# A hybrid decoder step on one core: per-layer products inside an expert group, and the two last norms applied behind the products

## The reference

```python
x = x + jnp.einsum("bld,de->ble", g_a * branch_a + g_b * branch_b, w_out)
hm = _rmsnorm(x, norm_ffn).reshape(b * l, D_MODEL)
x = x + _moe(hm, w_router, ...)            # top 4 of 32 experts, clamped SwiGLU, D_FF 1024
gate = jax.nn.sigmoid(jnp.einsum("bld,de->ble", _rmsnorm(x, norm_ple), w_ple_gate))
x = x + jnp.einsum("blp,pd->bld", p_l, w_ple_proj) * gate
y = _rmsnorm(x, norm_final)                # the two first outputs
# _rmsnorm(x, g) = x * rsqrt(mean(x * x) + 1e-6) * g
```

## Time and profile before

| | us |
|---|---|
| median of 3 runs | 1566.33 |
| lowest, highest | 1565.93, 1574.47 |
| the profiled execution | 1569.91 |
| its span, first to last instruction | 1568.2 |
| TensorE busy in it | 1411.7 |
| VectorE, ScalarE busy | 502.4, 248.5 |
| mean granted TensorE clock | 0.975 |

### The profile page before, as it was taken

One profiled execution on the slowest core, in us unless ns is written; L12 is line 12 of the kernel. 1 busy time (PEld: TensorE's weight loads), 2 busy tenths in 40 slices (PEclk: granted clock), 3 DMA queues, 4 the chain that ended last, 5 costly groups with the idle time before them and its releaser, 6 DMA issues.

```text
span 1568.2 us, 19774 instructions
## 1 busy us (share of the span) xinstructions
PE 1411.7 (90%) x7420; PEld 819.7 (52%) x7420; DVE 502.4 (32%) x1084; ACT 248.5 (16%) x495; POOL 49.6 (3%) x71
## 2 busy tenths in 40 slices
PE   3899999898999999988988988989989989989877
PEld 3587777676788843442442442443443443433356
DVE  1366677777522440220220220210210211211222
ACT  2351422314230300100100100100100100100022
POOL 2010001101000000000000000000000000000000
PEclk9899989999999999999999999999999999999989
DMA  6132323232249399999999999999999999999910
GB/s 187 41 121 68 116 65 112 80 107 86 67 128 369 131 377 421 421 422 422 421 422 421 421 421 422 421 422 422 422 420 421 420 423 421 422 422 422 399 45 28
DMA packets 120448, 462.67 MB, mean 295 GB/s; under 512 B 9783, under 2 KB 68680, under 8 KB 71128
## 3 DMA queue, kind: packets, MB, share of 16 engines
q1 hardware_dynamic: 100304, 447.97, 71.2%
q10 hardware_dynamic: 20080, 13.82, 3.1%
HBM read 455.75 MB, written 6.68 MB: 295 GB/s over the span
## 4 chain that ended last, share of the span: by engine, by line
PE 63%; DMA 21%; DVE 9%; ACT 2%; issue 2%; ACTq 1%; SPq 0%; POOL 0%; DVEq 0%; POOLq 0%
DMA ring<-in_w_gate_up 21%; PE bank L996 14%; PE bank L961 12%; PE bank L799 9%; PE bank L926 6%; PE bank L1017 4%; PE bank L843 3%; PE bank L671 2%; PE bank L1068 2%; PE bank L877 2%; DVE lent L1611 2%; PE bank L954 1%; ACTq L1099 1%; PE bank L609 1%; PE bank L677 1%
## 5 line engine op out<-in xcount | busy, mean ns | idle before, releaser
L961 PE MATMUL bank<-ring,lent 128*64 128x512 f32 (+1 forms) x2304 | 459.2, 595 | 73.6 <-DMA ring<-in_w_gate_up 73.4
L961 PEld LDWEIGHTS bank<-ring,lent 128*64 128x64 f32 (+1 forms) x2304 | 149.2, 131 | 371.7 <-issue 348.5
L799 PE MATMUL bank<-lent,ring 128*128 128x264 f32 x896 | 233.9, 406 | 2.9 <-DVE big L1632 1.6
L996 PE MATMUL bank<-ring,lent 128*64 128x512 f32 (+1 forms) x1152 | 226.7, 595 | 0.2 <-ACT lent L1367 0.2
L799 PEld LDWEIGHTS bank<-lent,ring 128*128 128x128 f32 x896 | 170.1, 200 | 36.9 <-issue 7.5
L1781 DVE TENSOR_SCALAR big<-bank 128x512 f32<-128x512 f32 x32 | 20.6, 686 | 431.4 <-PE bank L961 431.4
L996 PEld LDWEIGHTS bank<-ring,lent 128*64 128x64 f32 (+1 forms) x1152 | 69.8, 131 | 135.8 <-issue 128.7
L1361 ACT ACTIVATE big<-big 128x512 f32<-128x512 f32 x32 | 19.6, 630 | 549.1 <-DVE big L1781 549.1
L926 PEld LDWEIGHTS bank<-st,big 88*128 88x128 f32 x768 | 87.0, 192 | 12.7 <-issue 12.2
L926 PE MATMUL bank<-st,big 88*128 88x128 f32 x768 | 90.0, 277 | 0.1
L1799 DVE TENSOR_TENSOR xT<-xT,bank 128x264 f32<-128x264 f32 x128 | 55.0, 430 | 95.9 <-PE bank L1017 94.4
(11 more groups left out here) (328 smaller groups left out, 1127.8 us busy)
## 6 DMA issues: line engine op xcount, KB each, us to landing
ring<-in_w_gate_up SPq DMA_DIRECT2D x256, 1024.0 KB, 19.1
ring<-in_w_down SPq DMA_DIRECT2D x128, 1024.0 KB, 23.5
ring<-in_w_in SPq DMA_DIRECT2D x28, 1024.0 KB, 5.2
st<-in_state_gdn ACTq DMA_DIRECT2D x8, 512.0 KB, 4.3
out<-st ACTq DMA_DIRECT2D x8, 512.0 KB, 3.3
ring<-in_w_gdn_out SPq DMA_DIRECT2D x4, 1024.0 KB, 5.0
ring<-in_w_out SPq DMA_DIRECT2D x4, 1024.0 KB, 9.4
ring<-in_w_ple_gate SPq DMA_DIRECT2D x4, 1024.0 KB, 16.1
```

What stands on the lines that cost most here:

```text
L799: last = mm(b[:, 0:T], w[:, k, o:o + P], aT[:, k, :], start=k == 0, stop=k == KD - 1)
L961: last = mm(bank[t][lo:hi, :], x_slots[:, c, lo:hi], w, start=False, stop=c == KD - 1)
L996: last = mm(bank[4 + t][lo:hi, :], hT[:, m, lo:hi], w, start=m == 0, stop=m == KD - 1)
```

## The change

1. The per-layer products (pp) leave the end. In group index 13 (the fourteenth of 16, `PLE_GROUP`) TensorE runs the two products of one block behind each of the eight rounds, in banks 6 and 7; ScalarE copies each out of PSUM to pieces of SBUF that are free (pp_kept), and TensorE waits for the last copy ahead of the gather. The loops of TensorE and ScalarE are cut there. w_ple_proj gets a place in `lent` and is loaded by SyncE behind expert chunk 11, once the last block of w_out is out.
2. The gate's norm: TensorE multiplies xT * gain without rstd. VectorE multiplies the product by rstd when it leaves PSUM, ahead of the sigmoid. The sum of squares runs behind the first two gate blocks.
3. The final norm: squares are summed over blocks by VectorE as they come (sum3), the column sums are taken with tokens on the partitions (ss3), and the factor is applied as ScalarE and VectorE, three copies each, take the token rows out of PSUM.
4. The final transposes are no longer behind the second norm but between the gate blocks (`final_tokens`). They are of 88 tokens, three for a block.
5. TensorE, ScalarE and VectorE read the flag ahead of the last group; the branch stays where it is.
6. ScalarE loads its tables by dummy activations ahead of use (Sqrt before the root, Sigmoid after it, Sqrt after the last sigmoid). The stores of y are issued by SyncE, eight instead of six.

```diff
+PLE_GROUP = GROUPS - 3
+        w_ple = carve(lent, 2 * D + 2 * KD * SLOTS, 2, D)
+        for i, b in enumerate((1, 5, 6, 7, 1, 0, 1, 0)):
+            plan(f"pg{i}", b)
+        for h in range(2):
+            for t in range(NTB):
+                plan(f"y{t}{h}", 2 + 3 * h + t)
+        plan("ss3", 1)
...
+            to_drain(sp, f"wo{KD - 1}")
+            sp.dma_start(w_ple, a["w_ple_proj"][0].rearrange("(k p) d -> p k d", p=P)).then_inc(s["late_loaded"], 16)
             load_group(0, 0, loaded, first, True, RING, known=True)
...
+            def per_layer(i):
+                if i >= 2:
+                    pe.wait_ge(s["pp_kept"], i - 1)
+                for k in range(2):
+                    last = mm(aux[i % 2][:, 0:T], w_ple[:, k, i * P:(i + 1) * P], pT[:, k, :], start=k == 0, stop=k == 1)
+                last.then_inc(s["pp_filled"], 1)
...
+                if ple:
+                    pe.wait_ge(s["pp_kept"], KD)
                 if not last_one:
                     gather(sm, n + 1)
...
+            most = pe.value_load(flag[0:1, 0:1], min_val=0, max_val=MOST)
             group(first, loaded, slot_fills, GROUPS - 1, EVEN, False, True, True)
             last_scatter(first, GROUPS)
-            most = pe.value_load(flag[0:1, 0:1], min_val=0, max_val=MOST)
...
+            def final_tokens(k):
+
+                pe.wait_ge(s["xg_ready"], 2 * KD + k + 1)
+                for t in range(NTB):
+                    name = f"y{t}{k // 4}"
+                    b = to_fill(pe, name) if k % 4 == 0 else bank[uses[name][0]][:]
+                    x = tr(b[0:TB, (k % 4) * P:(k % 4 + 1) * P], x3g[:, k, t * TB:(t + 1) * TB], ident[:])
+                    if k % 4 == 3:
+                        fill_done(name, x)
+
+            gate_block(0)
+            gate_block(1)
+            sum_squares("rms3", 2)
+            gate_block(2)
+            gate_block(3)
+            final_tokens(0)
+            gate_block(4)
+            final_tokens(1)
+            final_tokens(2)
+            gate_block(5)
+            final_tokens(3)
+            gate_block(6)
+            final_tokens(4)
+            gate_block(7)
+            for k in range(5, KD):
+                final_tokens(k)
+            pe.wait_ge(s["squares"], 2 * KD + 2)
+            b = to_fill(pe, "ss3")
+            pe.wait_ge(s["squares3"], KD)
...
+            for k in range(KD):
+                act.wait_ge(first["sc_added"], GROUPS * KD - KD + k + 1)
+                A(aT[:, k, :], xT[:, k, :], ACT.Copy, scale=par[:, 16 + k:17 + k]).then_inc(s["xg_ready"], 1)
+            squares(zT, lambda k: None)
+            tell(A(small8[:, 3:4], small8[:, 0:1], ACT.Sqrt, scale=0.0))
             root(rstd[:], "rms3", 1.0 / D)
+            tell(A(small8[:, 3:4], small8[:, 0:1], ACT.Sigmoid))
             for i in range(KD):
+                wait_drained(act, f"pg{i}")
+                A(ple_gate[i % 2], ple_gate[i % 2], ACT.Sigmoid).then_inc(s["ple_sig"], 1)
+                if i == KD - 1:
+                    tell(A(small8[:, 3:4], small8[:, 0:1], ACT.Sqrt, scale=0.0))
+                act.wait_ge(s["x3"], i + 1)
+                if i < KD - 1:
+                    A(x3g[:, i, :], xT[:, i, :], ACT.Copy, scale=par[:, 24 + i:25 + i]).then_inc(s["xg_ready"], 1)
+                A(sq3[i % 2] if i else sum3, xT[:, i, :], ACT.Square).then_inc(s["squares3"], 1)
...
-            norm("rms3", 16)
+            wait_drained(dve, "rms3")
+            tell(v.reciprocal(rstd[:], rstd[:]))
             for i in range(KD):
+                b = to_drain(dve, f"pg{i}")
+                x = ple_gate[i % 2]
+                out_of(v.tensor_tensor(x, b[:, 0:T], rstd[:], ALU.mult), f"pg{i}")
+                if i >= 2:
+                    dve.wait_ge(s["squares3"], i)
+                    tell(v.tensor_tensor(sum3, sum3, sq3[(i - 1) % 2], ALU.add), "squares" if i == KD - 1 else None)
+                dve.wait_ge(s["ple_sig"], i + 1)
+                tell(v.tensor_tensor(x, x, pp[i], ALU.mult))
                 tell(v.tensor_tensor(xT[:, i, :], xT[:, i, :], x, ALU.add), "x3")
-            norm("rms4", 24)
+                if i == KD - 1:
+                    dve.wait_ge(s["xg_ready"], 3 * KD - 1)
+                    tell(v.tensor_scalar(x3g[:, i, :], xT[:, i, :], par[:, 24 + i:25 + i], None, ALU.mult), "xg_ready")
+            wait_drained(dve, "ss3")
+            tell(v.reciprocal(rstd_t, root_t), "rstd_ready")
+            for t in range(NTB):
+                b = to_drain(dve, f"y{t}1")
+                out_of(v.tensor_scalar(hm_tok[0:TB, t, 512:D], b[0:TB, :], rstd_t[:, t:t + 1], None, ALU.mult), f"y{t}1")
```

More of the change, by code:

```diff
@@ L1066, in _ @@
                     if i == 0:
[L1067 removed]
+                        pe.wait_ge(s["xg_ready"], KD + k + 1)
                     last = mm(b[:, 0:T], w[:, k, P * (i % 2):P * (i % 2) + P], aT[:, k, :], start=k == 0, stop=k == KD - 1)
                 fill_done(f"pg{i}", last)
[L1070 to L1073 removed]
@@ L1088, in _ @@
+            b = to_fill(pe, "ss3")
+            pe.wait_ge(s["squares3"], KD)
+            for t in range(NTB):
+                cols_t = slice(t * TB, (t + 1) * TB)
+                mm(b[0:TB, 2 * t:2 * t + 2], sum3[:, cols_t], ones[:, 0:2], start=True, stop=False)
+                last = mm(b[0:TB, 2 * t:2 * t + 2], sq3[1][:, cols_t], ones[:, 0:2], start=False, stop=True)
+            fill_done("ss3", last)
         @block.scalar
@@ L1371, in _ @@
             per = PAIR_ROUNDS * RING
-            with act.Fori(1, GROUPS - 1) as n:
-                group(first, n, n * per, False, False)
+            for lo, hi in ((1, PLE_GROUP), (PLE_GROUP, PLE_GROUP + 1), (PLE_GROUP + 1, GROUPS - 1)):
+                with act.Fori(lo, hi) as n:
+                    group(first, n, n * per, False, False, lo == PLE_GROUP)
+            most = act.value_load(flag[0:1, 0:1], min_val=0, max_val=MOST)
             group(first, GROUPS - 1, (GROUPS - 1) * per, False, True)
             outputs_of(first, GROUPS - 1, GROUPS * per)
-            most = act.value_load(flag[0:1, 0:1], min_val=0, max_val=MOST)
             with act.If(most > CAP):
@@ L1848, in _ @@
                     group(first, n, 2 * n, kind, after, 0, False, False)
+            most = dve.value_load(flag[0:1, 0:1], min_val=0, max_val=MOST)
             n = GROUPS - 1
```

99 lines of the change are left out of this document (41 added, 58 removed).

## The result

| | before | after |
|---|---|---|
| median, us (4 executions each, in turn) | 1570.4 | 1551.49 |
| lowest, highest | 1565.93, 1575.48 | 1548.72, 1554.01 |
| profiled execution | 1569.91 | 1548.72 |
| its span | 1568.2 | 1547.0 |

The ratio after to before is 0.9881, 95% interval 0.9854 to 0.9908: 18.9 us faster. Forecast were 21.4 less and 1544.9; the measured 1551.49 lies 1.0 us above the range. Five more rounds (experiment 1) gave 1553.51 against 1574.04, ratio 0.9873 [0.9851, 0.9896].

The account below looks back on a forecast made before the run. The weight stream bounds the kernel to 1461.5 us, then engines waiting for one another. Hole 0.35, TensorE's stretch 11.95 and tail 9.1 sum to 21.4 us: 1566.33 to 1544.9, range 1539.5 to 1550.5.

Parts of the forecast that it names:

- (b): Hole behind the last scatter: the flag's read was most of it, 0.8 us stays, 4.9 us less, 1540.0; chance 0.13.
- (d): Gate blocks: hand-overs between engines set the pace, costing above 3.9 us a gate; at 4.9, 6 us more, 1551; chance 0.06.
- (e): Gate stretch: TensorE's clock stays at 1.2 GHz throughout, 31 us more than the sum, 1576; chance 0.02.
- the base: Last step of the sum: the profiled execution's 3.6 us over the median carries over, so 21.4 comes off 1566.33, giving 1544.9.
- I take that it does, once: Behind the last scatter: a hole of 3.0 us brings TensorE's clock down once, costing 2.6 to 2.7 us.
- (a): Behind the last scatter: the hole stays but the clock does not fall, 2.7 us less, 1542.2; chance 0.22.
- hole stays 3.0: TensorE behind the last scatter: of 3.35 us idle, 3.0 stay, mostly the branch; reading the flag earlier gains 0.35.
- I take 0, bounds 0 and 2.6: Weight stream, fourteenth group: the added products make TensorE late, but the next group makes it up; cost 0, at most 2.6 us.
- the new loops for single groups are like those that the uneven groups have already: Weight stream: cutting loops to give single groups their own loop bodies was taken to cost 0.
- (c): Weight stream gives time back through the 1 MB load or the fourteenth group's 2.6 us; up to 5.1 more, 1550.0; chance 0.12.
- Gate stretch 33.7: TensorE from the hole to the last gate block's end: eight blocks, squares and five transposes' delays, 33.7 us without a clock fall.
- Tail 10.2: From the last gate block's end to the kernel's end: 10.2 us against 19.3 before, 9.1 less.

Follow-up runs that it names:

- experiment 1: Both kernels rerun without edit: the changed kernel 1553.51 us against 1574.04, ratio 0.9873; later the kernel before, 1566.68 us, ratio 0.9987 to its other executions.
- after again: The changed kernel, no edit, timed in five more rounds against the kernel before and profiled a second time: median 1553.51 us, ratio 0.9873.

## Why the prediction was right or wrong

**Direction and place: right.** Each of the parts showed where it was put: one hole behind the scatter, no bracket between gate blocks, products that cost the stream nothing by themselves. Rivals (b), (d) and (e) are refuted: no hole of 0.8, no stall in eight blocks, no lasting slow clock.

**The step that failed for the time is the last of the sum, the base:** "That execution took 1569.91 ... 3.6 over the median; the difference carries over, so 1566.33 - 21.4 = 1544.9." The sum was made against a profile with two falls of the clock, and then put on a median of executions that were quicker than that one. In the comparison the median of before was 1570.4, 4.1 above 1566.33; the time missed the forecast by 6.6 us, and these 4.1 are the larger part of it, the gain of 18.9 instead of 21.4 the other 2.5. From the profile's own time the sum gives 1548.5, where 1548.72 was measured; that is luck in part, since the errors cancel and both profiles have the short S. What the range lacked was a term for the base: before lies in two clusters 8 us apart, and three executions do not say in what shares. Part of that difference is S (4.2 us), part the falls in the two holes of the end (3.5 us between the two profiles of before); and the second part does not carry over, since the change alters those very holes. On the pooled median of before, 1572.3, the same 21.4 gives 1550.9, within 0.6 us of the result.

**The gain itself** was 18.9 us, not 21.4; in the five later rounds it was 20.5. Both figures depend on how many executions of either kernel had the long S. By end - S the means of the two profiles each are 941.4 and 922.7, a gain of 18.6. The terms, as the prediction put them:

- *"I take that it does, once"* (the clock falls, 2.7): wrong for what was profiled. In after and after again the hole of 2.80 and 2.24 us left the clock up, as in seven of the eight profiles with the flag read early. Rival (a) was right about that, its 0.22 too low, unless the middle four of the nine executions of after did have a fall (experiment 1).
- *"hole stays 3.0"*: right in kind, a little long. The branch is most of the hole, and reading the flag some 0.7 of it; 2.2 to 2.8 stayed.
- *Stream, "I take 0, bounds 0 and 2.6":* 1.3, and for a reason that no rival named. The lateness was seen rightly in kind: it is made up in the next group. Its size was not, 3.8 us instead of 2.6, since the rounds took 4.68 us and not 4.5. But "the new loops for single groups are like those that the uneven groups have already" put them at nothing: their code has to be fetched, by engines that were full. The page of before shows 43 such fetches, of after 46, and the 38th comes at 1341 instead of 1465, ahead of the stream's end. Rival (c) has the size, not the cause.
- *Gate stretch 33.7:* 33.76.
- *Tail 10.2:* 12.7. The drain of 1.38 us that the Trainium skill adds to a table load ("ScalarE: Activation LUTs", What ACT_TABLE_LOAD costs) does not show here: the load starts 0.02 us behind the sigmoid (1535.02 + 0.42), and its dummy 0.01 behind the load. Copies start at T + 5.0, not 4.7, and the first store at T + 5.7, not 5.4; then the last of eight stores was to start 2.9 us behind the first, and the end to come 1.9 behind that. It was 4.2 and 2.8. Both prices came from rows in which the DMA engines had little to do or the shape was another (loads, and one store at a time from ScalarE); now eight were issued back to back, four of them 88 rows wide, where before wrote rows of 128. This is the term that cost the gain most.

In the profiled pair the missing fall (-2.6) and the longer tail (+2.5) cancel. Against the second profile of before, which has no fall in its first hole either, they don't: the 106.64 that the sum started from is 102.62 there.

## What to carry to other kernels

Put a forecast on the execution from which it was summed, compare its clock falls with those of the other times shown, and give the base a term in the range when only three executions are known. Where a stream fills the DMA engines, further loop bodies are not free: count the instruction fetches ahead of the stream's end. And when stores end a kernel, choose their rows so that all DMA engines take part, and hide a branch under a wait that is there anyway.

## What was not expected of the hardware

- Every eighth fetch of TensorE's code (the 30th, 38th, 46th) put 0.8 to 1.6 us into a stream at 421 GB/s, mostly some 1.35. The others put in 0.3 at most, and once 0.55.
- The first half of the kernel ends at one of two moments, 4.2 us apart, in both kernels. In the eleven later ones the granted clock was 0.66 or 0.67 from 150 to 160 us, in the seven earlier ones 1.00.
- A branch over code that is not run costs TensorE 2.2 to 2.8 us (3.8 in one of eight profiles), and 0.1 to 0.9 in four of five profiles when it stands ahead of a wait of 1.2 (1.4 in the fifth).
- Stores of 88 and 80 rows ran at 182 to 275 GB/s, those of 128 at 373 to 385.
- The table load at the tail took 1.28 us, with the engine idle for 0.02 ahead of it and 0.01 behind.
